# Third head's query one position later in the first head, and the first latents' head's query products behind the weighted sums of positions five and six

## The chip, the core and the metric

The kernel runs on one core of a Trainium2 chip. Its engines work through queues of their own, in the order written in the program, and wait for each other by semaphores: TensorE (PE, matmuls and their weight loads PEld), VectorE (DVE), ScalarE (ACT), GpSimd (POOL, which here issues the gathers) and SyncE (SP, which issues the other transfers). The metric is the time of one execution in microseconds of the device; less is better.

## The reference

One layer of a backbone over 128 context tokens and 512 latent tokens, D = 1024: a modulated RMS norm, a mixer (state space and short convolution), a residual, and then the part in which the change lies, a retrieval of single-neuron experts:

```python
def block(xb):                                   # 128 tokens
    q = (xb @ w_query).reshape(TOKEN_BLOCK, PEER_HEADS, 2, PEER_DQ // 2)
    s = jnp.einsum("thse,sne->thsn", q, sk)      # scores of 2 x 128 keys
    s1, i1 = lax.top_k(s[:, :, 0], PEER_TOPK)
    s2, i2 = lax.top_k(s[:, :, 1], PEER_TOPK)
    cand = s1[..., :, None] + s2[..., None, :]   # 16 x 16 sums
    ...
    top, pos = lax.top_k(cand, PEER_TOPK)
    idx = jnp.take_along_axis(cidx, pos, axis=-1)
    gate = jax.nn.softmax(top, axis=-1)
    hid = jnp.einsum("thkd,td->thk", expert_u[idx], xb)
    act = jax.nn.gelu(hid) * gate
    return jnp.einsum("thk,thkd->td", act, expert_v[idx])
```

There are 8 heads, 16 experts for each token and head, and five blocks of 128 tokens: the context and four of latents. The context's block runs first.

## The kernel before

After a first part of some 210 us (modulation, mixer of the context, scans) one long loop does the retrieval: `for G in range(NALL)`, 40 turns, one for each block and head, G = 8 b + head. In this text "first head" is G = 0, "seventh head" G = 6, and so on. Each turn has 8 positions g, and each position handles two of a token's 16 experts. Every engine has the same double loop, written out by hand, and what stands in it sets the order of its queue.

- **GpSimd** (L1861) gathers one expert row for each of 128 tokens, 8 KB each (the u half and the v half together), into one of 8 row slots. It waits for the experts of the head (`topk_done`) and for its slot, which is free when the weighted sum of the expert 8 places before is done (`v_done`). The sum of position g frees two slots, so the sums of positions 4 to 7 admit the first eight gathers of the next head.
- **VectorE**: for each expert k, `dot` (L1678) multiplies the row's u half with the token; every second k, `weigh` (L1690) writes the weights of the position before. Between them stand the stages of the next head's top-k, from `best_keys` (L1619, top keys, ahead of dot 0, it waits for the key scores) to `take_experts` (L1663, ahead of dot 8, in the first head dot 10), which reads what TensorE has spread, and, in the first eight heads, the latents' mixer (`latent_front`, among them L1725 and L1739). The weight of position 7 is written in the next head, behind its top keys and dot 0.
- **ScalarE**: a Gelu for each position (L1228), and the evictions of query and scores: `take_q`, `take_scores` (L1203, L1209) for the context's heads, `take_q_lat`, `take_scores_lat` (L1213 to L1220) for the latents'.
- **TensorE**: at each position `add_rows` (L846), the weighted sum of two experts' v halves; `spread_experts` (L832); `latent_front` (L908 to L934) for the latents' mixer in the first six heads; and the query of the head after the next, u = G + 2, in two halves (`query`, L781; `query_lat`, L814) and its key scores (`scores`, L801; `scores_lat`, L823). For the latents one query head serves all 512 tokens; the first of these is u = 8, in the seventh head. It needs the latents' normed tokens, which ScalarE's modulation (L1082) finishes in position 4 of that head.
- **SyncE** loads w_query head by head into one buffer: the next load waits until both halves of the query before have been computed. The tiles of the latents' weights stand in the same queue.

The position in which a query half stands is fixed by `g in (3, 4)` and `g in (4, 5)` in the loops: it stands ahead of the position's weighted sum. The scores stand in position 6.

Of the kernel before, what the change touches and what calls it, by code (L numbers as in the profile page):

```python
# [37 lines left out]
HEADS = 8  # L38
# [41 lines left out]
def build(nc, xT, condT, cols, w_mod, w_u, w_tiles, w_o, ssm, bc, dskip, skT, w_query, table, y_out, st_out, kfull):  # L80
    ctx = ExitStack()
    with ctx:
# [276 lines left out]
        NQC = 2 * HEADS  # L359
# [122 lines left out]
        def _(pe):  # L482
# [171 lines left out]
            for i in range(4):  # L654
                for term in range(5):
                    r = (term - 1) // 2
                    for a in range(2):
                        for j in range(4):
                            g = 8 * j + 2 * i + a
# [115 lines left out]
            def query(u, halves=range(2)):  # L775

                pe.wait_ge(ld_wq, 16 * u)
                pe.wait_ge(sc_ev, u)
                for h in halves:
                    for k in range(KD):  # L780
                        last = mm(bank[2][:, h * P:(h + 1) * P], wqb[:, k, h * P:(h + 1) * P], hT[:, k, 0:CTX], start=(k == 0), stop=(k == KD - 1))  # L781
                if h == 1:
                    last.then_inc(q_mm, 1)
# [33 lines left out]
            def scores_lat(u):  # L817

                n = u - HEADS
                pe.wait_ge(lq_ev, 2 * n + 2)  # L820
                for j in range(4):
                    for h in range(2):
                        last = mm(bank[2 + j // 2][:, (j % 2) * DQ + h * P:(j % 2) * DQ + (h + 1) * P], qTl[:, h, j * P:(j + 1) * P], sk[:, h, :],  # L823
                                  start=True, stop=True)
                last.then_inc(sc_mm, 1)
# [187 lines left out]
            for G in range(NALL):  # L1013
                b, head = G // HEADS, G % HEADS
                t, u = G + 1, G + 2
                for g in range(NPR):
                    if g == (2 if G else 4) and t < NALL:
                        spread_experts(t)
                    if u < HEADS:
                        if g in (3, 4):  # L1020
                            query(u, (g - 3,))
                        if g == 6:
                            scores(u)
                    if HEADS <= u < NQC:
                        if g in (4, 5):
                            query_lat(u, g - 4)
                        if g == 6:
                            scores_lat(u)
                    add_rows(G, g)
                    if G == 0 and g == 0:  # L1030
                        turn_y(2)
                        turn_y(3)
                    if b == 0:
                        latent_front(NPR * G + g)
                    if head == HEADS - 1 and b < NBLK - 1:
                        if g == 1:
                            turn_rows(b + 1)
                        for tg in HID_AT.get(g, ()):
                            select_group(b + 1, tg)
                    if head == 0 and b and g == 2:  # L1040
                        turn_sums(b - 1)
                    if head == 1 and b and g == 1:
                        final_squares(b - 1)
                    if G == NALL - 5 and g in (1, 3):
                        last_rows(g // 2)
# [5 lines left out]
        def _(act):  # L1051
# [273 lines left out]
            for G in range(NALL):  # L1325
                b, head = G // HEADS, G % HEADS
                e, t, u = G % 2, G + 1, G + 2
                for g in range(NPR):
                    if g == (1 if G else 3) and t < NALL:
                        exps(t)  # L1330
                    if u < HEADS:
                        if g == 5:
                            take_q(u)
                        if g == 6:
                            take_scores(u)
                    gelu(G, e, g)
                    if G == 0 and g == 0:
# [2 lines left out]
                    if b == 0:  # L1340
                        latent_front(NPR * G + g)
                    if HEADS <= u < NQC:
                        if g in (4, 5):
                            take_q_lat(u, g - 4)
                        if g == 6:
                            take_scores_lat(u)
                    if head == HEADS - 1 and b < NBLK - 1:
                        if g == 2:
# [577 lines left out]
```

## Time and profile before

| | us |
|---|---|
| timed executions, median of 3 (1967.2 to 1967.95) | 1967.68 |
| profiled execution, whole | 1977.83 |
| its span, first to last instruction | 1976.0 |
| TensorE busy (61%) | 1196.6 |
| VectorE busy (73%) | 1441.2 |
| ScalarE busy (19%) | 375.7 |
| GpSimd busy (36%) | 719.9 |

The gathers move 671.13 of the 745.90 MB; the slices in the second half of the span show 413 to 421 GB/s, mostly near 417, but for the last. TensorE's mean granted clock is 0.699. The profile knows each instruction by line, engine and operation, with the time it started, how long it took, and in brackets how long its engine had been idle before and what released it. In windows each engine has its busy time and count, then come the granted TensorE clock (1.00 is 2.4 GHz, 0.50 is 1.2 GHz), the DMA share and GB/s. A matmul of the program shows as two in the trace.

### The profile page before, as it was taken

Reading aid. Unit: us, or ns where it says so; the run is one execution under the profiler, and the core shown is the slowest. Engines: PE = TensorE matmul, PEld = TensorE weight load, DVE = VectorE, ACT = ScalarE, POOL = GpSimd, SP = SyncE. Lnnn points to the kernel's source line nnn. Section 1 sums busy time; section 2 is a strip of 40 time slices with the busy share of each in tenths; the row PEclk is TensorE's granted clock in tenths of the full one; section 3 lists DMA queues with packets and bytes.
Section 4 is the critical chain, followed back from the end, with each engine's and each line's share of the span. In section 5 each row is a group of like instructions: output and inputs, shape, how many; then the busy total and the mean of one; then the engine's idle time right before and its main releaser. Section 6 shows DMA issues by size and latency. Waiting matters only on the chain.

```text
span 1976.0 us, 22252 instructions
## 1 busy us (share of the span) xinstructions
PE 1196.6 (61%) x7540; PEld 460.7 (23%) x7540; DVE 1441.2 (73%) x3894; ACT 375.7 (19%) x845; POOL 719.9 (36%) x666
## 2 busy tenths in 40 slices
PE   6999888988767666775544434464434454444444
PEld 3569533333323222221101000021000011011001
DVE  8977566877766776666788777777777777876765
ACT  5232431221222111111221011121111111211110
POOL 0000332333333433433443444444344444344442
PEclk9999998999878777776655555565555566555555
DMA  8556799999989999999999999999999999999996
GB/s 347 173 202 227 279 367 344 377 376 387 396 330 384 389 397 388 397 403 372 420 417 421 421 414 416 420 407 419 413 413 419 410 413 410 416 417 411 414 417 255
DMA packets 126242, 745.90 MB, mean 377 GB/s; under 512 B 12128, under 2 KB 34912, under 8 KB 40624
## 3 DMA queue, kind: packets, MB, share of 16 engines
q0 software_dynamic: 92160, 671.13, 83.2%
q1 hardware_dynamic: 33968, 73.35, 10.4%
q8 instruction: 59, 0.97, 0.2%
q14 instruction: 55, 0.45, 0.1%
HBM read 741.78 MB, written 2.65 MB: 377 GB/s over the span
## 4 chain that ended last, share of the span: by engine, by line
DMA 34%; PE 29%; DVE 24%; issue 10%; ACT 1%; SPq 0%; DVEq 0%; POOL 0%; POOLq 0%; ACTq 0%
DMA r<-table,gidx 30%; DVE r L1678 8%; PE bank L846 7%; PE bank L814 6%; DMA r<-w_query 3%; PE bank L923 3%; PE bank L934 2%; PE bank L543 2%; DMA r<-w_u 2%; DVE wgt L1690 1%; PE bank L781 1%; DVE r L1646 1%; DVE i L1620 1%; DVE i L1626 1%; DVE r L1621 1%
## 5 line engine op out<-in xcount | busy, mean ns | idle before, releaser
L1861 POOL DMA_INDIRECT r<-table,gidx x640 | 711.7, 1112 | 1072.8 <-PE bank L846 911.2
L1678 DVE CUSTOM_DVE_ANT_0 r<-r 128x1024 f32<-128x1024 f32 x640 | 780.0, 1224 | 302.7 <-DMA r<-table,gidx 273.9
L846 PE MATMUL bank<-r,wgt 128*32 128x512 f32 x2560 | 536.0, 923 | 729.3 <-DVE wgt L1690 710.5
L846 PEld LDWEIGHTS bank<-r,wgt 128*32 128x32 f32 x2560 | 61.5, 131 | 1103.4 <-DVE wgt L1690 1033.6
L1228 ACT ACTIVATE r<-r 128x2 f32<-128x2 f32 x320 | 65.1, 203 | 1046.5 <-DVE r L1678 1038.6
L814 PE MATMUL bank<-hT_r,r 128*128 128x512 f32 x256 | 123.6, 639 | 0.9 <-ACT hT_r L1082 0.9
L1687 DVE TENSOR_TENSOR r<-r 128x2 f32<-128x2 f32 x320 | 50.1, 157 | 92.3 <-ACT r L1228 92.3
L1690 DVE TENSOR_TENSOR wgt<-fold,r 128x64 f32<-128x64 f32 x320 | 72.0, 225 | 11.1
L814 PEld LDWEIGHTS bank<-hT_r,r 128*128 128x128 f32 x256 | 51.3, 206 | 77.6 <-issue 77.6
L1228 ACT ACT_TABLE_LOAD x51 | 65.4, 1283 | 0.9
L923 PE MATMUL bank<-hT_r,r 128*128 128x512 f32 x128 | 62.2, 631 | 0.0
L934 PE MATMUL bank<-mix_r,r 128*128 128x512 f32 x128 | 61.2, 621 | 0.0
L832 PEld LDWEIGHTS bank<-r,ident 128*32 128x32 f32 x1280 | 43.0, 139 | 48.8 <-DVE r L1657 42.7
L1678 DVE DVE_READ_ACCUMULATOR2_ANT r<- 128x1 f32 x640 | 52.9, 83 | 0.0
L1224 ACT ACT_TABLE_LOAD x40 | 51.3, 1283 | 0.7
L871 PE MATMUL bank<-mix_r,modrow 128*128 128x512 f32 x80 | 48.0, 737 | 3.2 <-ACT r L1243 1.9
L832 PE MATMUL bank<-r,ident 128*32 128x8 f32 x1280 | 46.8, 195 | 3.9 <-DVE r L1657 3.6
L1846 POOL MEMSET r<- 128x2048 f32 x1 | 1.8, 1813 | 93.2 <-DVE sv L1477 93.2
L1619 DVE MAX8 r<-r 128x8 f32<-128x128 f32 x80 | 19.3, 284 | 22.0 <-ACT r L1220 15.9
L1224 ACT ACTIVATE r<-r,small 128x16 f32<-128x16 f32 x40 | 12.3, 308 | 119.9 <-DVE pos L1639 119.9
L781 PE MATMUL bank<-hT_r,r 128*128 128x128 f32 x224 | 29.5, 289 | 7.2 <-DMA r<-w_query 7.2
L543 PE MATMUL bank<-hT_r,r 128*128 128x512 f32 x64 | 32.0, 646 | 2.2 <-DMA r<-w_u 2.2
(356 smaller groups left out, 1431.4 us busy)
## 6 DMA issues: line engine op xcount, KB each, us to landing
r<-w_mod SPq DMA_DIRECT2D x24, 1024.0 KB, 8.4
r<-w_query SPq DMA_DIRECT2D x15, 1024.0 KB
r<-table,gidx POOLq DMA_INDIRECT x640
r<-w_tiles SPq DMA_DIRECT2D x12, 512.0 KB, 6.7
x_r<-w_tiles SPq DMA_DIRECT2D x10, 512.0 KB, 5.8
hT_r<-xT SPq DMA_DIRECT2D x4, 640.0 KB, 6.2
r<-w_u SPq DMA_DIRECT2D x1, 2048.0 KB, 30.5
r<-w_o SPq DMA_DIRECT2D x1, 2048.0 KB, 11.1
```

The lines of the kernel that those rows point to most:

```text
L543: last = mm(bank[m][:, :], wu[:, k, m * P:(m + 1) * P], hT[:, k, CTX:T], start=(k == 0), stop=(k == KD - 1))
L814: last = mm(bank[2 + h][:, :], wqb[:, k, h * P:(h + 1) * P], hT[:, k, CTX:T], start=(k == 0), stop=(k == KD - 1))
L832: last = mm(bank[3][TG * s:TG * s + TG, 8 * tg:8 * tg + 8], ident[:, TG * tg:TG * tg + TG], gi[:, :, 4 * s:4 * s + 4], start=True, stop=True)
L846: last = mm(bank[ACC[b % 2][h]][to:to + TG, :], wgt[:, g % 2, e, :], rows[:, k % SLOTS, D + h * 512:D + (h + 1) * 512], start=(G % HEADS = ...
L923: last = mm(bank[(4, 5, 7)[r]][:, :], wtl[(tile + 2) % 3][:, k, :], hT[:, k, CTX:T], start=(k == 0), stop=(k == KD - 1))
L934: last = mm(bank[OUT_BANK[m % 3]][:, :], woA[:, m % 4, k, :], mixl[:, k, :], start=(k == 0), stop=(k == KD - 1))
L1224: A(e16, top, ACT.Exp, bias=small[:, 0:1], accum_out=small[:, 1:2]).then_inc(exp_done, 1)
L1228: A(gel[:, par, 2 * g:2 * g + 2], hid[:, par, 2 * g:2 * g + 2], ACT.Gelu_apprx_tanh).then_inc(gelu_done, 1)
L1678: V.tensor_tensor_reduce(rows[:, s, 0:D], rows[:, s, 0:D], h2r[tg], 1.0, 0.0, ALU.mult, ALU.add, hid[:, par, k:k + 1]).then_inc(dot_done, 1)
L1687: wl(tt(a, a, gate[:, par, 2 * g:2 * g + 2], ALU.mult))
L1690: tt(wgt[:, g % 2, :, :], fold[:, :].rearrange("p (a m) -> p a m", a=1).broadcast_to([P, 2, TG]), a.rearrange("p (g m) -> p g m", m=1).bro ...
L1861: G_.indirect_dma_start(rows[:, k % SLOTS, :], None, table, bass.IndirectOffsetOnAxis(gidx[:, e, k:k + 1], 0)).then_inc(row_in[k % SLOTS], 16)
```

## The change

Two things move, on TensorE and on ScalarE. In the first head the halves of the third head's query (u = 2) go from positions 3 and 4 to 4 and 5, its eviction from 5 to 6, its scores and their eviction from 6 to 7. In the seventh head the halves of the first latents' query (u = 8) go from ahead of the sums of positions 4 and 5 to behind those of 5 and 6, the scores from position 6 to 7; ScalarE takes the two halves in positions 6 and 7, behind the Gelus of these, and the scores in 7. Other heads keep their places, and no instruction is added or left out.

```diff
                     if u < HEADS:
-                        if g in (3, 4):
-                            query(u, (g - 3,))
-                        if g == 6:
+                        q0 = 3 if G else 4
+                        if g in (q0, q0 + 1):
+                            query(u, (g - q0,))
+                        if g == q0 + 3:
                             scores(u)
-                    if HEADS <= u < NQC:
+                    if HEADS < u < NQC:
                         if g in (4, 5):
                             query_lat(u, g - 4)
                         if g == 6:
                             scores_lat(u)
+                    if u == HEADS and g == 7:
+                        scores_lat(u)
                     add_rows(G, g)
+                    if u == HEADS and g in (5, 6):
+                        query_lat(u, g - 5)
...
                     if u < HEADS:
-                        if g == 5:
+                        q0 = 3 if G else 4
+                        if g == q0 + 2:
                             take_q(u)
-                        if g == 6:
+                        if g == q0 + 3:
                             take_scores(u)
...
                     if HEADS <= u < NQC:
-                        if g in (4, 5):
-                            take_q_lat(u, g - 4)
-                        if g == 6:
+                        q0 = 4 if u > HEADS else 6
+                        if g in (q0, q0 + 1):
+                            take_q_lat(u, g - q0)
+                        if g == max(q0 + 1, 6):
                             take_scores_lat(u)
```

TensorE's queue in the first head, before, from the product of position 2 (L908) to that of position 4 (L912, L923); L781 is a query half, L846 a weighted sum, L832 the spreading of the experts:

```order
L908 MATMUL bank<-r 128x512 [waits sgl_ev]
L908 MATMUL bank<-r 128x512 x3
L781 MATMUL bank<-hT_r,r 128x128 [waits sc_ev,ld_wq]
L781 MATMUL bank<-hT_r,r 128x128 x7
L846 MATMUL bank<-r,wgt 32x512 [waits wgt_ready]
L846 MATMUL bank<-r,wgt 32x512 x3
```

The difference at the same place, of the changed kernel against the one before, at the scores (L801):

```order
 L912 MATMUL bank<-r,ones 128x512 [waits sql_ready]
 L923 MATMUL bank<-hT_r,mix_r 128x512 x4
-L801 MATMUL bank<-sk,r 128x128 [waits q_ev]
-L801 MATMUL bank<-sk,r 128x128
 L846 MATMUL bank<-r,wgt 32x512 [waits wgt_ready]
 L846 MATMUL bank<-r,wgt 32x512 x3
```

Of the first piece the two L781 rows are gone in the changed kernel, so the sum of position 3 follows the product of position 2; the halves now follow the products of positions 3 and 4. The scores leave their place ahead of the sum of position 6 and stand ahead of that of position 7.

TensorE's queue in the seventh head, before, from the first half (L814) to the scores (L823):

```order
L814 MATMUL bank<-hT_r,r 128x512 [waits h_ready,sc_ev,ld_wq]
L814 MATMUL bank<-hT_r,r 128x512 x7
L846 MATMUL bank<-r,wgt 32x512 [waits wgt_ready]
L846 MATMUL bank<-r,wgt 32x512 x3
L814 MATMUL bank<-hT_r,r 128x512 [waits topk_done]
L814 MATMUL bank<-hT_r,r 128x512 x7
L846 MATMUL bank<-r,wgt 32x512 [waits wgt_ready]
L846 MATMUL bank<-r,wgt 32x512 x3
L823 MATMUL bank<-sk,r 128x128 [waits lq_ev]
L823 MATMUL bank<-sk,r 128x128 x7
```

And in the changed kernel, from the sums of positions 4 and 5 to the scores:

```order
L846 MATMUL bank<-r,wgt 32x512 [waits wgt_ready]
L846 MATMUL bank<-r,wgt 32x512 x3
L846 MATMUL bank<-r,wgt 32x512 [waits wgt_ready]
L846 MATMUL bank<-r,wgt 32x512 x3
L814 MATMUL bank<-hT_r,r 128x512 [waits h_ready,sc_ev,ld_wq]
L814 MATMUL bank<-hT_r,r 128x512 x7
L846 MATMUL bank<-r,wgt 32x512 [waits wgt_ready]
L846 MATMUL bank<-r,wgt 32x512 x3
L814 MATMUL bank<-hT_r,r 128x512 [waits topk_done]
L814 MATMUL bank<-hT_r,r 128x512 x7
L823 MATMUL bank<-sk,r 128x128 [waits lq_ev]
L823 MATMUL bank<-sk,r 128x128 x7
```

Two sums stand ahead of the first half, one between the halves, and none between the second half and the scores, which wait for ScalarE's eviction of that half (`lq_ev`).

ScalarE's queue in the seventh head, before, from the last modulation (L1082); L1213 takes a half, L1228 is a Gelu, L1217 begins the eviction of the scores:

```order
L1082 ACTIVATE hT_r<-hT_r,modT,gs 128x512
L1213 ACTIVATE r<-bank 128x512 [waits lq_mm]
L1228 ACTIVATE r<-r 128x2 [waits dot_done]
L1213 ACTIVATE r<-bank 128x512 [waits lq_mm]
L1228 ACTIVATE r<-r 128x2 [waits dot_done]
L1217 ACTIVATE r<-bank 128x512 [waits sc_mm]
```

The same in the changed kernel, where these lines are five further down:

```order
L1087 ACTIVATE hT_r<-hT_r,modT,gs 128x512
L1233 ACTIVATE r<-r 128x2 [waits dot_done] x2
L1218 ACTIVATE r<-bank 128x512 [waits lq_mm]
L1233 ACTIVATE r<-r 128x2 [waits dot_done]
L1218 ACTIVATE r<-bank 128x512 [waits lq_mm]
L1222 ACTIVATE r<-bank 128x512 [waits sc_mm]
```

The Gelus of positions 5, 6 and 7 each go ahead of an eviction that they followed before.

## Rows read from the trace of the kernel before

**Rows 1.** The page: DMA share by slice; the chain that ended last, by line.

```profile
DMA  8556799999989999999999999999999999999996
...
DMA r<-table,gidx 30%; DVE r L1678 8%; PE bank L846 7%; PE bank L814 6%; DMA r<-w_query 3%; PE bank L923 3%; PE bank L934 2%; PE bank L543 2%; DMA r<-w_u 2%; DVE wgt L1690 1%; PE bank L781 1%; DVE r L1646 1%; DVE i L1620 1%; DVE i L1626 1%; DVE r L1621 1%
```

**Rows 2.** First head, TensorE: start us, busy us, line, [idle before <- releaser].

```profile
243.65 3.70 PE L908 MATMUL bank<-r 128*128 128x512 f32 x8
251.62 2.80 PE L781 MATMUL bank<-hT_r,r 128*128 128x128 f32 x16 [4.27 <-DMA r<-w_query]
254.35 1.93 PE L846 MATMUL bank<-r,wgt 128*32 128x512 f32 x8
...
259.84 0.88 PE L832 MATMUL bank<-r,ident 128*32 128x8 f32 x32
...
262.67 1.07 PE L846 MATMUL bank<-r,wgt 128*32 128x512 f32 x8
...
268.15 1.07 PE L846 MATMUL bank<-r,wgt 128*32 128x512 f32 x8
...
273.54 0.61 PE L801 MATMUL bank<-sk,r 128*128 128x128 f32 x4
...
280.65 1.06 PE L846 MATMUL bank<-r,wgt 128*32 128x512 f32 x8
```

**Rows 3.** First head, VectorE: a weight, experts taken, top keys, product.

```profile
248.08 0.23 DVE L1690 TENSOR_TENSOR wgt<-fold,r 128x64 f32<-128x64 f32 x1
...
260.75 0.17 DVE L1663 COPY r<-bank 128x16 f32<-128x16 f32 x1 [10.70 <-PE bank L832]
...
276.18 0.48 DVE L1619 MAX8 r<-r 128x8 f32<-128x128 f32 x2
...
286.32 0.69 DVE L1739 TENSOR_TENSOR r<-r,bank 128x512 f32<-128x512 f32 x1 [0.42 <-PE bank L923]
```

**Rows 4.** First head, windows: busy by engine, granted clock, DMA share, GB/s.

```profile
253.00:254.00 1.00, 1.00 (x6) 1.00 (x6) 0.00 (x0) 0.00 (x0) 0.00 (x0) 0.50 1.02 422
254.00:269.00 15.00, 15.00 (x92) 6.54 (x91) 7.87 (x18) 3.70 (x6) 5.45 (x4) 0.93 0.80 289
```

**Rows 5.** Seventh head, TensorE in order of time.

```profile
562.18 9.37 PE L814 MATMUL bank<-hT_r,r 128*128 128x512 f32 x16 [0.95 <-ACT hT_r L1082]
571.48 1.06 PE L846 MATMUL bank<-r,wgt 128*32 128x512 f32 x8
...
580.54 2.05 PE L823 MATMUL bank<-sk,r 128*128 128x128 f32 x16
...
587.37 1.93 PE L846 MATMUL bank<-r,wgt 128*32 128x512 f32 x8 [3.78 <-DVE wgt L1690]
```

**Rows 6.** Seventh head, VectorE in order of time.

```profile
561.64 0.23 DVE L1690 TENSOR_TENSOR wgt<-fold,r 128x64 f32<-128x64 f32 x1
...
564.60 1.23 DVE L1678 CUSTOM_DVE_ANT_0 r<-r 128x1024 f32<-128x1024 f32 x1 [1.60 <-DMA r<-table,gidx]
...
583.87 0.49 DVE L1619 MAX8 r<-r 128x8 f32<-128x128 f32 x2 [1.94 <-ACT r L1220]
```

**Rows 7.** Seventh head, ScalarE: second eviction of the query.

```profile
579.65 0.60 ACT L1213 ACTIVATE r<-bank 128x512 f32<-128x512 f32 x1 [7.37 <-PE bank L814]
```

**Rows 8.** Seventh head, window from the first query half into the second.

```profile
570.00:577.50 7.50, 7.50 (x24) 2.92 (x23) 2.67 (x6) 0.69 (x2) 2.30 (x2) 1.00 0.52 188
```

**Rows 9.** Eighth head, TensorE: the tenth head's two query halves.

```profile
608.63 7.03 PE L814 MATMUL bank<-hT_r,r 128*128 128x512 f32 x16
...
618.40 7.03 PE L814 MATMUL bank<-hT_r,r 128*128 128x512 f32 x16
```

**Rows 10.** Eighth head, window behind the second half.

```profile
625.00:627.50 2.50, 1.83 (x11) 0.46 (x10) 0.30 (x2) 1.67 (x4) 0.28 (x1) 1.00 0.56 215
```

**Rows 11.** Eighth head, VectorE: a dot product that waits for rows.

```profile
612.31 1.23 DVE L1678 CUSTOM_DVE_ANT_0 r<-r 128x1024 f32<-128x1024 f32 x1 [2.39 <-DMA r<-table,gidx]
```

**Rows 12.** Twelfth head, TensorE: a first query half behind the fourth sum.

```profile
793.06 8.30 PE L814 MATMUL bank<-hT_r,r 128*128 128x512 f32 x16
```

## The prediction

> **What bounds the kernel now.** I read the page first. Its DMA strip stands at 9 from the sixth of its 40 slices on, but for the last and the twelfth, which holds the seventh head. The chain that ended last is 30% gathers of table rows, but TensorE's weighted sums (L846) and query halves (L814) are 7% and 6% of the span on it [rows 1]. So I looked at who waits for whom at the two places the change touches, and not at the sums over the span.
>
> In the first head the two query halves of the third head stand in TensorE's queue behind the products of positions two and three. The first half waits 4.27 us for the load of w_query, with the sum of position three queued behind it [rows 2], although that sum's weight was written at 248.3 us [rows 3]. The idle time costs again afterwards: the granted clock is 0.50 in 253 to 254 us, the 1.2 GHz level [rows 4], and the half takes 2.80 us. VectorE meanwhile stands 10.70 us before it can take the next head's experts [rows 3], since their spreading comes only at 259.84 us [rows 2].
>
> In the seventh head VectorE does not wait for rows at the end: it waits for the key scores. The first query half of the ninth head starts at 562.18 us, released by ScalarE's modulation, and from there TensorE runs without a gap through sum 4, half two, sum 5 and the scores at 580.54 [rows 5]. ScalarE takes the scores, VectorE starts the top keys at 583.87 [rows 6], and the weight of sum 7 stands behind these top keys and one dot product, so sum 7 starts at 587.37 [rows 5]. VectorE then never waits for rows up to the eighth head's sum 3, and TensorE goes on from there into the query halves at 608.63 and 618.40 [rows 9]. **That is one unbroken chain** from 562 to 625 us; what delays the first half delays everything behind it. The gathers are not its bound: between 570 and 577.5 us the DMA share is only 0.52 [rows 8].
>
> **Place one, the first head.** The two halves go one position later, the key scores from position six to seven, and ScalarE's evictions with them. I walk the new queue with the old durations. Sum 3 starts at 248.4 (weight at 248.3 [rows 3]) and takes 1.0; the product of position three takes 3.70 [rows 2], end 253.1. Spreading and one half took 2.83 (259.84 to 262.67 [rows 2]): end 255.9. VectorE takes the experts at 254.0 instead of 260.75 and needs 1.9 to the weight (it did so in the trace, sum 4 at 262.67 being ready then), so sum 4 starts at 256.0, against 262.67. Its latent product (262.67 to 268.15 is sum plus product, 5.5) ends at 261.4, the second half 2.0 later at 263.4, sum 5 with its product 5.4 later (268.15 to 273.54 [rows 2]) at 268.9, sum 6 with its product 5.5 later at 274.4, and then the scores. They stood at 273.54 and now stand at 274.4: **the 4.27 us of idle and 1.6 us of slow clock are saved, but the product of position six, 4.5 us, now runs ahead of the scores.** The scores end at 275.0, ScalarE copies in 0.5, VectorE starts the top keys at 275.5, against 276.18 [rows 3], where it was held by a dot product. Sum 7 stands behind the top keys, a dot product and its weight; from the start of the top keys to sum 7 the seventh head has 3.5 (583.87 to 587.37 [rows 5, 6]), so it starts at 279.0 against 280.65. TensorE idles 4.0 us for it, nearly as long as the gap that was followed by the 0.50 clock [rows 2, 4], and that gap cost 1.6 or 1.7 (2.80 on the half against 2.0, 1.93 on the sum against 1.07). So the product that VectorE waits for at 286.32 [rows 3] comes at 280.65 − 1.65 + 1.65 + its 5.5, just when it came before: **place one comes out even, 0.0 us**. Ends: −1.1 if the clock stays high (VectorE's own chain is 0.7 early and its 0.42 wait goes), +1.5 if the slow stretch covers all of the product (3.70 at the high clock). I take 0.0, since the gap is nearest to the 4.27 us one. The next load of w_query and the weight tiles are released by the same products and come some 4 us earlier on SP; nobody waited for them there.
>
> The Trainium skill ("TensorE: Matmul & The Clock Gate", section "Loop structure matters more than you think") says that a wait between bursts of matmuls drops the clock to half. The 0.50 clock after the 4.27 us wait agrees. By it the change trades one such gap for another; without it place one would give −1.1 and the sum 1971.2.
>
> **Place two, the seventh head.** Sums 4 and 5 now stand ahead of the first half. Sum 4 has its weight at 561.9 [rows 6] and takes 1.9 at the low clock. Sum 5 needs the dot products of rows 10 and 11, a Gelu, and, by VectorE's order, the dot product of row 12, which waits for its gather until 564.60 and ends at 565.8 [rows 6]; its weight is there at 566.2. Sum 5 ends at 568.2. **The first half starts there, 6.0 us later than 562.18.** It may be shorter than 9.37, since TensorE has worked before it: in the twelfth head, where sum 3 runs at the low clock right ahead of it and no half waits for a modulation, it took 8.30 [rows 12]. That is −1.1, with ends 0 (9.37 again [rows 5]) and −2.3 (7.03, as in the eighth head [rows 9]). Between the first half and the scores stood two sums and one half, 571.48 to 580.54 or 9.1 us [rows 5]; now stand one sum (1.0), one half (7.1), and ScalarE's copy of the second half, 0.60 [rows 7] and 0.1 of handing over, which sum 5 used to cover: 8.8, so −0.3. The sum is 6.0 − 1.1 − 0.3 = **+4.6 us** at the scores, bounds +3.4 and +5.7. Scores, their copy, the top keys, one dot product and the weight up to sum 7 stay 6.8 us (580.54 to 587.37 [rows 5]): sum 7 starts at about 592.0.
>
> What is won there: sums 4 and 5 free row slots 7 and 11 us earlier, so six of the eighth head's gathers are early and the empty DMA stretch at 572 fills. But sums 6 and 7 come at 576.5 and 592.0 instead of 582.52 and 587.37, and the gathers behind sum 7 with them; between these the DMA runs dry instead. ScalarE's Gelus of positions five to seven no longer stand behind the evictions, yet VectorE only idles longer before the scores.
>
> **Sum.** 0.0 + 4.6 = +4.6 us on a span of 1976.0 us, 1.83 us of the 1977.83 us of the profiled execution lying around it. The timed ones have a median of 1967.68, 10.15 us less; the difference is carried over unscaled: 1967.68 + 4.6 = **1972.3 us**, 0.23% slower. Behind the tenth head's halves the DMA share is again only 0.56 [rows 10]: few gathers are outstanding there in either order, so from there on everything is the same but later, and a delay is carried on as it is.
>
> **Rivals.** *The DMA alone counts, and it gets faster.* The share is 0.80 over 254 to 269 [rows 4] and 0.52 over 570 to 577.5 [rows 8]: 15 × 0.20 + 7.5 × 0.48 = 3.0 + 3.6 = 6.6 us of empty DMA. If early gathers fill that and stay ahead to the end, the time is 1967.68 − 6.6 = 1961.1. It decides if the backlog built in the early gathers outlasts the wait for sum 7. Six gathers cannot: a gather is 128 rows of 8 KB, 1.05 MB, which is 2.5 us at the 417 GB/s of the full slices, so six are through by some 587 and sum 7's two are asked for at 594. The Trainium skill ("Perfetto Trace Analysis", section "Identifying the Most-Contended Engine") says to improve the most contended engine first; that is this rival's rule with the DMA as that engine. The trace speaks against it here: while the share is 0.52, VectorE waits for ScalarE and TensorE, not for rows [rows 6]. Chance 0.11.
>
> *The delay of place two is absorbed.* In the eighth head VectorE waits for rows, 2.39 us for one of them [rows 11], so it could be 4.6 us late and lose little; 0 to 2 us would be left, say 1.1, 1968.8. Against it: the path to the tenth head's halves [rows 9] leads over sum 3, which does not wait for rows. Chance 0.16.
>
> *Place one keeps its whole saving.* If the scores were not behind a product, 4.3 + 1.6 = 5.9 us would be saved there, total +4.6 − 5.9, 1966.4. Chance 0.07.
>
> *More slow clock*: +1.5 and +5.7 at the two places, and some more where a shifted head meets the low clock: beyond 1975, to 1978. Chance 0.08.
>
> **How the numbers follow.** The forecast has 0.58; its own range is −1.1 + 3.4 = +2.3 to 1.5 + 5.7 = +7.2, so 1970.0 to 1974.9. A measurement of this kernel tells 0.2%, 3.9 us, from no change, so the part of the forecast below 1971.6, a fourth of it, falls to "same". Faster: 0.11. Same: 0.16 + 0.07 + 0.14 = 0.37. Slower: 0.44 + 0.08 = 0.52. The range 1966 to 1976 leaves out the first rival and the far end of the last, about 0.15.
>
> **What would show it.** Place one: sum 3 at 248.4, experts taken at 254, the scores of the third head near 274.4 and an idle gap of 4 us before sum 7 at 279.0, with a clock of 0.50 shortly behind. Place two: sum 5 done at 568, the first half at 568 to 576.5, scores at 585, top keys at 588.5, sum 7 at 592, all shifted by what place one gives; a dry DMA near 588 to 594. It would be wrong if the tenth head's halves did not start some 4.6 us later than 608.63 and 618.40 [rows 9]; if they are later and the end is not, the second rival has it further on.

## The result

The changed kernel takes 1980.03 us (median of 7, 1972.81 to 1981.72), the kernel before 1967.95 (median of 7, 1966.73 to 1971.14). The ratio is **1.0044, 95% interval 1.0028 to 1.0061**, which is +8.7 us (5.5 to 12.0) on 1967.95. It is slower, as the likeliest case had it, but by about twice the forecast 4.6 us, and the median lies 4 us above the range. The profiled execution took 1980.33 us, its span is 1978.5 us. All ratios of this document are of fast runs; one slow execution of the kernel before, 5193.41 us in the last series, is left out of them.

The page of the changed kernel: clock and DMA by slice, then the chain that ended last, by line:

```profile
PEclk9999998999978777776655555565555566555555
...
DMA  8456798999998999999999999999999999999996
...
DMA r<-table,gidx 30%; DVE r L1685 8%; PE bank L846 7%; PE bank L814 6%; PE bank L923 3%; PE bank L934 2%; PE bank L543 2%; DMA r<-w_query 2%; DVE wgt L1697 1%; PE bank L781 1%; DVE r L1653 1%; DVE i L1627 1%; DVE r L1628 1%; DVE i L1633 1%; DVE pos L1641 1%
```

Against [rows 1] nearly nothing moves: a share of 1% is 20 us here, so the page cannot show this change. The hollow in the DMA strip's twelfth slice stands in the thirteenth (593 to 643 us). The two places have to be read row by row. (In the changed kernel VectorE's lines are 7 higher, L1697 writes the weights and L1685 is the dot product; ScalarE's are 5 higher.)

**First head**, TensorE in order of time:

```profile
251.01 1.06 PE L846 MATMUL bank<-r,wgt 128*32 128x512 f32 x8 [1.02 <-DVE wgt L1697]
...
256.45 2.05 PE L781 MATMUL bank<-hT_r,r 128*128 128x128 f32 x16
263.86 1.95 PE L781 MATMUL bank<-hT_r,r 128*128 128x128 f32 x16
...
273.18 3.60 PE L923 MATMUL bank<-hT_r,r 128*128 128x512 f32 x8
276.61 0.61 PE L801 MATMUL bank<-sk,r 128*128 128x128 f32 x4
281.56 1.93 PE L846 MATMUL bank<-r,wgt 128*32 128x512 f32 x8 [4.34 <-DVE wgt L1697]
283.42 2.08 PE L912 MATMUL bank<-r,ones 128*128 128x512 f32 x2
285.29 4.10 PE L923 MATMUL bank<-hT_r,r 128*128 128x512 f32 x8
```

The wait for w_query of [rows 2] is gone. The product of position six stands ahead of the scores (L801), TensorE then idles 4.34 us for the weight behind the top keys. The sum that follows and the first part of its product (L912 in 2.08 us for 1.13, L923 in 4.10 for 3.60) run at the low clock. The window shows it (busy by engine, clock, DMA share, GB/s), where [rows 4] had the same behind the wait for w_query:

```profile
281.00:285.00 4.00, 3.44 (x10) 1.04 (x11) 3.62 (x16) 1.05 (x2) 0.72 (x1) 0.50 0.99 375
```

**Seventh head**, TensorE, to be set beside [rows 5]:

```profile
564.16 1.94 PE L846 MATMUL bank<-r,wgt 128*32 128x512 f32 x8 [0.68 <-DVE wgt L1697]
568.31 1.94 PE L846 MATMUL bank<-r,wgt 128*32 128x512 f32 x8 [2.21 <-DVE wgt L1697]
570.17 8.53 PE L814 MATMUL bank<-hT_r,r 128*128 128x512 f32 x16
578.63 1.06 PE L846 MATMUL bank<-r,wgt 128*32 128x512 f32 x8
579.63 7.13 PE L814 MATMUL bank<-hT_r,r 128*128 128x512 f32 x16
587.45 2.05 PE L823 MATMUL bank<-sk,r 128*128 128x128 f32 x16 [0.69 <-ACT r L1218]
594.28 1.93 PE L846 MATMUL bank<-r,wgt 128*32 128x512 f32 x8 [4.78 <-DVE wgt L1697]
```

VectorE at its top keys, beside the 1.94 us of [rows 6], and the windows over the first half (0.52 in [rows 8]) and between scores and sum 7:

```profile
590.79 0.49 DVE L1626 MAX8 r<-r 128x8 f32<-128x128 f32 x2 [14.16 <-ACT r L1225]
```

```profile
587.00:594.00 7.00, 2.05 (x16) 1.86 (x16) 2.93 (x14) 1.54 (x4) 0.00 (x0) 0.96 0.75 281
570.00:577.50 7.50, 7.50 (x18) 3.33 (x15) 4.00 (x8) 0.20 (x1) 3.14 (x3) 0.80 1.01 423
```

The early gathers fill the empty stretch (0.52 becomes 1.01), and VectorE, with its rows in place, idles 14.16 us for the scores. The emptiness has moved: the share is 0.75 in 587 to 594 us and 0.84 over 593 to 643, where the kernel before has 1.02 in 587 to 594 and 0.97 over 594 to 643. The filled stretch is worth little, because the head ends when the scores come.

### The profile page after: what moved, and what is told of

It is laid out like the page before. It is cut to its first block, busy times and chain, and to the rows that moved or that the text cites. A ratio compares the mean times of both kernels' runs of the same rounds, so it can differ in the third digit from the quotient of the medians.

```text
span 1978.5 us, 22252 instructions
## 1 busy us (share of the span) xinstructions
PE 1200.5 (61%) x7540; PEld 461.9 (23%) x7540; DVE 1441.6 (73%) x3894; ACT 376.5 (19%) x845; POOL 720.4 (36%) x666
## 4 chain that ended last, share of the span: by engine, by line
DMA 32%; PE 30%; DVE 25%; issue 11%; ACT 2%; POOL 0%; DVEq 0%; POOLq 0%; SPq 0%; ACTq 0%
DMA r<-table,gidx 30%; DVE r L1685 8%; PE bank L846 7%; PE bank L814 6%; PE bank L923 3%; PE bank L934 2%; PE bank L543 2%; DMA r<-w_query 2%; DVE wgt L1697 1%; PE bank L781 1%; DVE r L1653 1%; DVE i L1627 1%; DVE r L1628 1%; DVE i L1633 1%; DVE pos L1641 1%
## 5 line engine op out<-in xcount | busy, mean ns | idle before, releaser
L1685 DVE CUSTOM_DVE_ANT_0 r<-r 128x1024 f32<-128x1024 f32 x640 | 780.1, 1224 | 307.2 <-DMA r<-table,gidx 289.8
L846 PE MATMUL bank<-r,wgt 128*32 128x512 f32 x2560 | 539.8, 928 | 735.6 <-DVE wgt L1697 716.9
L846 PEld LDWEIGHTS bank<-r,wgt 128*32 128x32 f32 x2560 | 61.6, 130 | 1112.6 <-DVE wgt L1697 1043.3
L814 PE MATMUL bank<-hT_r,r 128*128 128x512 f32 x256 | 118.7, 618 | 0.0
L1697 DVE TENSOR_TENSOR wgt<-fold,r 128x64 f32<-128x64 f32 x320 | 72.0, 225 | 11.1
L814 PEld LDWEIGHTS bank<-hT_r,r 128*128 128x128 f32 x256 | 49.5, 199 | 73.1 <-issue 73.1
L923 PE MATMUL bank<-hT_r,r 128*128 128x512 f32 x128 | 62.5, 633 | 0.0
L832 PEld LDWEIGHTS bank<-r,ident 128*32 128x32 f32 x1280 | 43.5, 140 | 48.9 <-DVE r L1664 42.7
L1685 DVE DVE_READ_ACCUMULATOR2_ANT r<- 128x1 f32 x640 | 52.9, 83 | 0.0
L871 PE MATMUL bank<-mix_r,modrow 128*128 128x512 f32 x80 | 48.8, 748 | 3.2 <-ACT r L1248 1.9
L832 PE MATMUL bank<-r,ident 128*32 128x8 f32 x1280 | 47.4, 196 | 3.7 <-DVE r L1664 3.6
L1229 ACT ACTIVATE r<-r,small 128x16 f32<-128x16 f32 x40 | 12.4, 309 | 121.4 <-DVE pos L1646 121.4
L923 PEld LDWEIGHTS bank<-hT_r,r 128*128 128x128 f32 x128 | 24.7, 202 | 38.9 <-issue 38.9
L934 PEld LDWEIGHTS bank<-mix_r,r 128*128 128x128 f32 x128 | 23.7, 195 | 38.3 <-issue 36.6
```

The source lines that it names most:

```text
L814: last = mm(bank[2 + h][:, :], wqb[:, k, h * P:(h + 1) * P], hT[:, k, CTX:T], start=(k == 0), stop=(k == KD - 1))
L832: last = mm(bank[3][TG * s:TG * s + TG, 8 * tg:8 * tg + 8], ident[:, TG * tg:TG * tg + TG], gi[:, :, 4 * s:4 * s + 4], start=True, stop=True)
L846: last = mm(bank[ACC[b % 2][h]][to:to + TG, :], wgt[:, g % 2, e, :], rows[:, k % SLOTS, D + h * 512:D + (h + 1) * 512], start=(G % HEADS = ...
L871: last = mm(bank[at[h]][:, :], modrow[:, tg // 2, tg % 2 * P:(tg % 2 + 1) * P], h2tok[:, 512 * h:512 * h + 512], start=True, stop=True)
L923: last = mm(bank[(4, 5, 7)[r]][:, :], wtl[(tile + 2) % 3][:, k, :], hT[:, k, CTX:T], start=(k == 0), stop=(k == KD - 1))
L934: last = mm(bank[OUT_BANK[m % 3]][:, :], woA[:, m % 4, k, :], mixl[:, k, :], start=(k == 0), stop=(k == KD - 1))
```

## The experiments

All are read with one ruler: the start of the weighted sum (L846) of each position. "Step 0.2" is the time from the start of sum 2 of the first head to that of sum 3; "first head" is from sum 0 of the first head to sum 0 of the second. A second ruler is the timed ratio to the kernel before, taken on the same chip. Segments in us, spans of the traced executions:

```
trace           first heads  seventh heads    span
                head  2 - 6   head  8 - 14
before          55.5  253.1   54.1   321.1   1976.0
again_before    56.0  248.6   54.5   321.4   1972.6
before_trace    52.9  246.6   54.1   318.0   1967.0
before_trace2   54.6  249.8   53.7   318.7   1969.1
place1_only     56.1  251.8   54.6   319.3   1975.4
place1_trace    59.9  248.7   54.6   319.1   1976.7
place1_trace2   57.5  251.6   54.8   318.5   1976.3
place2_only     54.2  249.1   58.8   318.5   1972.2
place2_trace    50.7  252.3   58.5   316.9   1973.1
after           57.4  252.1   58.8   314.9   1978.5
again_after     57.5  248.7   59.1   315.1   1971.6
after_trace2    56.8  249.3   58.6   317.0   1976.2
after_trace3    55.9  252.1   58.7   318.0   1978.6
scores_late     62.2  246.6   54.0   317.4   1972.5
halves_late     56.0  250.3   54.3   319.4   1973.8
halves_q6       51.8  251.4   54.1   321.0   1971.3
half_behind4    52.8  246.0   54.9   318.5   1966.4
early_both      51.8  250.8   55.1   315.1   1968.5
```

From the fifteenth head to the end all 18 take 1061.0 to 1063.4 us: what is lost or won by then stays so.

**The two kernels again**, unedited, as the yardstick.

> The kernel before itself, for a second trace and for what the measurement tells from no change. Both theories: ratio 1.000, interval within 0.2%. If the profiled execution of before was a long one (1977.83 against a median of 1967.95), this trace has a span near 1966, and the 10 us lie in the tenth to fourteenth heads, where the two traces at hand come back together by 6.3 us. If they are the profiler's, the span is near 1976 again.

> The changed kernel itself again. Theory A (the delay at place two, 4.7 us in the trace, is carried to the end and nothing else costs): +5 us, 1973. Theory B (the first measurement holds, +8.7 us or more: something behind place two costs again): 1976 to 1980.

Measured: the kernel before against itself 1971.64 to 1968.39, 1.0013 (0.9999 to 1.0026); the changed one 1983.59 to 1968.39, 1.0069 (1.0047 to 1.0092). The loss is real, and on this chip larger than either theory had it (1973, or 1976 to 1980). The expectation for the kernel before failed too: its span is 1972.6 us for 1966, and heads 8 to 14 take 321.4 us, no less than in the first trace, so the long execution is not long there. The kernel before ran from 1962.96 to 1976.51 us in 23 executions, so a single trace is off the median by up to 8 us in either direction.

**Each place alone.**

```diff
 # place1_only: the first-head part of the change (ScalarE's part of it too)
-                        if g in (3, 4):
-                            query(u, (g - 3,))
-                        if g == 6:
+                        q0 = 3 if G else 4
+                        if g in (q0, q0 + 1):
+                            query(u, (g - q0,))
+                        if g == q0 + 3:
                             scores(u)
...
 # place2_only: the seventh-head part (ScalarE's part of it too)
+                    if u == HEADS and g == 7:
+                        scores_lat(u)
                     add_rows(G, g)
+                    if u == HEADS and g in (5, 6):
+                        query_lat(u, g - 5)
```

> Only the first head's part, the third head's query one position later; the seventh head as before. Forecast of the prediction: 0.0 us, -1.1 to +1.5. Rival (it keeps its saving of idle): -3 us or more. Theory B with its cost here: +3 to +4 us.

> Only the seventh head's part, the first latents' query behind sums five and six. Forecast: +4.6 us. If absorbed: 0 to +2. If its delay puts the later heads into a longer rhythm, +7 to +10.

Measured: place one alone 1977.23 to 1968.39, **1.0051** (1.0033 to 1.0069); place two alone 1974.29, **1.0029** (1.0015 to 1.0042). Place two costs +5.7 us, and its interval (3.0 to 8.3) holds the forecast 4.6. Place one, forecast at 0.0, costs +10.0 us (6.5 to 13.6). That is the miss.

**Which part of place one.** Two runs split it: the halves late but the scores only one position behind the eviction, and the scores late alone.

```diff
 # halves_late (scores stay at 6, ScalarE's take_q at 5)
-                        if g in (3, 4):
-                            query(u, (g - 3,))
+                        q0 = 3 if G else 4
+                        if g in (q0, q0 + 1):
+                            query(u, (g - q0,))
...
 # scores_late, on TensorE and ScalarE
-                        if g == 6:
+                        if g == (6 if G else 7):
```

> The first head's query halves one position later as in the change, but the scores and their eviction stay in position 6; ScalarE takes the query in position 5; seventh head as before. Theory A (what costs at place one is the product that now runs ahead of the scores): the scores come 4 us earlier than in the changed kernel, the first head's end 3 to 5 us before that of the kernel before, ratio 0.998. Theory B (what costs is the halves or the earlier transfers behind them): slower, as the first head's part alone was, 1.005.

> Only the third head's scores and their eviction move from position 6 to 7 of the first head, the halves stay where they were. Theory A: this has the whole cost and none of the saving, so sum 0 of the second head comes 4 to 6 us later than in the kernel before, ratio 1.003 to 1.005. Theory B: no change in time.

Measured: halves_late 1975.28 to 1971.09, 1.0017 (1.0003 to 1.0031); scores_late 1973.96, 1.0018 (1.0004 to 1.0032). Neither ratio is one that a theory named: halves_late was to be 0.998 or 1.005, scores_late 1.003 to 1.005 or no change. The two losses are little larger than the 1.0013 between two series of one kernel, so the traces have to decide. The late scores give the longest first head of all, 62.2 us, and leave the wait for w_query where it was. TensorE there:

```profile
252.49 3.38 PE L781 MATMUL bank<-hT_r,r 128*128 128x128 f32 x16 [4.90 <-DMA r<-w_query]
...
279.87 0.61 PE L801 MATMUL bank<-sk,r 128*128 128x128 f32 x4
284.82 1.93 PE L846 MATMUL bank<-r,wgt 128*32 128x512 f32 x8 [4.34 <-DVE wgt L1690]
```

The 4.34 us gap and the low clock come from the scores standing behind the product of position six: here the halves are in their old places, and both are there. From sum 3 to sum 0 of the second head it takes 37.3 us for 31.3, the 4 to 6 us of Theory A. halves_late has a price of its own. On ScalarE the eviction of the query waits for the second half and holds back the Gelu of position five behind it (L1229), which also pays 1.28 us for a table load. VectorE's weight comes late and sum 5 waits 2.44 us; the product behind it is 1.7 us longer than in halves_q6 below, at the low clock:

```profile
265.98 0.38 ACT L1204 ACTIVATE r<-bank 128x256 f32<-128x256 f32 x1 [8.89 <-PE bank L781]
266.38 1.28 ACT L1229 ACT_TABLE_LOAD   x1
267.67 0.20 ACT L1229 ACTIVATE r<-r 128x2 f32<-128x2 f32 x1
```

**Both costs taken out of place one.** Halves at 4 and 5 as in the change, scores ahead of sum 6, and ScalarE takes the query in position six, behind the Gelu of position five, as in the change:

```diff
 # halves_q6: halves_late, and
-                        if g == 5:
+                        if g == (5 if G else 6):
                             take_q(u)
```

> First head only: the query halves in positions 4 and 5, the scores stay in position 6 ahead of its sum, and ScalarE takes the query in position 6 too, so no Gelu stands behind a half. Theory A (place one costs because the scores wait for one more product and sum 7 for them): this has no such wait, sum 0 of the first head to sum 0 of the second takes 50 to 53 us where the changed kernel's traces have 57 and those of before 53 to 56; ratio 0.997 to 1.000. Theory B (any later half costs, through what it does to the transfers): 1.003 or more.

Measured 1968.87 to 1969.89, 0.9997 (0.9985 to 1.0009): the loss of place one is gone, the halves are as late as in the change. TensorE:

```profile
272.92 1.06 PE L846 MATMUL bank<-r,wgt 128*32 128x512 f32 x8 [1.02 <-DVE wgt L1691]
...
278.41 1.07 PE L846 MATMUL bank<-r,wgt 128*32 128x512 f32 x8
...
283.89 1.06 PE L846 MATMUL bank<-r,wgt 128*32 128x512 f32 x8
```

With the scores ahead of sum 6, that sum and its product cover VectorE's top keys. The gap is 1.02 us and the clock stays high (1.00 over 270 to 284 us). This is Theory A's first head (51.8 us for 50 to 53) and its ratio; Theory B's 1.003 lies outside the interval.

**A dose for place two.** The first half behind sum 4 only, the second behind sum 5, the scores back at position six:

```diff
 # half_behind4 (the halves leave their place ahead of the sums; ScalarE takes them in 5 and 6)
...
                     add_rows(G, g)
+                    if u == HEADS and g in (4, 5):
+                        query_lat(u, g - 4)
```

> Seventh head only, half as far as the change: the first query half behind sum 4, the second behind sum 5, scores in position 6 ahead of sum 6, ScalarE takes the halves behind the Gelus of 5 and 6. By the walk of the prediction the scores come 1.3 us later than before, where the change has 4.7. Chain theory: ratio 1.0005. Rival (the seventh head's empty DMA counts): faster, since sum 4 frees its slots 7 us early and there is no wait for sum 7.

Measured 1970.27 to 1971.09, 1.000 (0.9984 to 1.0016). The seventh head takes 54.9 us, 0.5 more than the old order's 54.3:

```profile
553.48 1.94 PE L846 MATMUL bank<-r,wgt 128*32 128x512 f32 x8 [0.69 <-DVE wgt L1694]
555.34 8.81 PE L814 MATMUL bank<-hT_r,r 128*128 128x512 f32 x16
564.08 1.07 PE L846 MATMUL bank<-r,wgt 128*32 128x512 f32 x8
565.07 7.13 PE L814 MATMUL bank<-hT_r,r 128*128 128x512 f32 x16
572.89 2.05 PE L823 MATMUL bank<-sk,r 128*128 128x128 f32 x16 [0.69 <-ACT r L1216]
```

Sum 4's weight is there after an idle 0.69 us. The half behind it starts 24.6 us after the head's start, 1.6 later than in [rows 5], and takes 8.81 us for 9.37; the scores are 0.8 us late (42.1 for 41.3), where 1.3 were expected. Sum 5's weight comes 4.15 us after sum 4 starts (564.16 to 568.31 in the changed kernel), and a half that stands behind it pays for that: in the changed kernel the first half starts 28.7 us after the head's start. So it is mainly the wait for sum 5 that costs, as the chain has it. (The second half and the scores are one position earlier here too, so the run does not part these from the first half.)

**More traces**, to see how much of one trace is that execution.

> The kernel before again, one look for a third trace. The timed executions of it have a median near 1968, the two traces at hand 1974 and 1978. If the traced ones are drawn from the same executions, this one is near 1968, and the place where it is shorter shows where executions of one kernel differ: the steps between weighted sums that differ by 2 us or more between traces (fourth head, positions 2 to 3, and second head, 2 to 3).

> The kernel before, a fourth trace. If a wait for w_query ahead of sum 3 and a low clock right behind sum 0 exclude each other, this trace has one of them: either a wait of 2 to 4 us and 54 to 56 us for the first head, or none, the product of position 0 at the low clock, and about 53 us and a span near 1967.

> The first head's part alone, a second trace. Theory A: from sum 0 of the first head to that of the second 56 to 58 us, 2 to 4 more than before, whatever the clock does; the heads behind, whose code is unchanged, 249 to 252 us up to the seventh as in the first trace and both of the changed kernel's. If these are chance alone, they may be at 246.

> The seventh head's part alone, a second trace. The seventh head 58.8 us against 54.1 to 54.5 of before in every trace; the seven heads behind it 315 to 319 us against 318 to 321: a part of the delay is given back there. If it isn't, 320.

> The changed kernel, one more look. If the loss of place one lies in the first head alone: from the first weighted sum of head one to that of head two 56 to 60 us (the kernel before 51 to 56), steps after sums 3, 4, 5 and 6 of 7.27, 5.49, 10.34 and 7.8 to 8.2 us whatever the time of the execution; heads two to six 246 to 253 us as in the kernel before, the seventh 58.8, heads 8 to 14 315 to 318. If executions above 1980 us hold a further loss, it shows as a segment outside these bounds.

> The changed kernel again, for the same question: the same steps in the first and the seventh head to within 0.5 us, and whatever differs between this execution and the others outside them is the spread of the unchanged heads (in the kernel before, 246.0 to 253.1 us for heads two to six).

> The move in the first head alone. First head 56 to 60 us, seventh head 54.1 to 54.6, heads 8 to 14 318 to 321. If the loss beyond +4 us lies in heads two to six, these stand above 250 us here too; if it is the spread of executions, they fall anywhere from 246 to 253.

These executions took 1968.83, 1970.86, 1978.45, 1974.95, 1978.00, 1980.43 and 1978.11 us. Most segments fall where they were expected; outside by over 0.3 us are the first head of place1_trace (59.9 us for 56 to 58) and step 0.7 of after_trace2 (7.17 for 7.8 to 8.2). The steps of the first head settle place one (old order: the four traces of before, two with place two alone, half_behind4; place one: seven traces):

```
step                     0.2                                 0.3        0.4   0.5    0.6       0.7
old order   6.41 6.41 6.41 9.49 10.11 11.70 12.52   7.45 to 8.39   5.48  7.02   5.48      5.49
place one   5.71 in all seven                       7.45           7.27  5.49  10.34  7.17 to 8.18
```

Steps 0.3 to 0.7 are the same in all seven traces with place one, but for the last, and together 7.1 us longer than in the old order (38.4 against 31.3). What pays for it is step 0.2, and that differs from execution to execution: in three of seven old-order traces the query half does not wait for w_query at all. In the trace of before that took 1968.83 us, TensorE in order of time, and a window:

```profile
233.74 1.94 PE L846 MATMUL bank<-r,wgt 128*32 128x512 f32 x8 [3.30 <-DVE wgt L1690]
...
238.84 5.92 PE L908 MATMUL bank<-r 128*128 128x512 f32 x8 [1.27 <-ACT r L1249]
...
253.85 1.95 PE L781 MATMUL bank<-hT_r,r 128*128 128x128 f32 x16
255.73 1.07 PE L846 MATMUL bank<-r,wgt 128*32 128x512 f32 x8
```

```profile
234.00:244.00 10.00, 8.73 (x23) 3.85 (x16) 9.29 (x28) 3.32 (x4) 1.86 (x2) 0.53 1.05 404
```

Here the clock falls early, behind sum 0, and products zero and one end later. That looks like the reason why the half finds w_query loaded, but it is not: the load itself was quick. From its issue to its landing the load of w_query took 15.9 us in this trace, so it landed near 244.3 us, 9.5 before the half, and the slow stretch is 3.6 us. The two other traces without a wait have 16.9 and 18.1 us. In the trace of before that took 1970.86 us the load took 25.4 us. The load in the two traces of before (issue, size, us from issue to landing):

```profile
r<-w_query SPq DMA_DIRECT2D x1, 1024.0 KB, 15.9
r<-w_query SPq DMA_DIRECT2D x1, 1024.0 KB, 25.4
```

In the second of these both stand together, a low clock behind sum 0 and a wait for w_query, which the expectation had as excluding each other; place two's second trace has a slow sum 0 and no wait. TensorE in these two traces:

```profile
230.16 1.91 PE L846 MATMUL bank<-r,wgt 128*32 128x512 f32 x8 [3.30 <-DVE wgt L1690]
...
250.28 3.40 PE L781 MATMUL bank<-hT_r,r 128*128 128x128 f32 x16 [2.09 <-DMA r<-w_query]
```

```profile
233.66 1.94 PE L846 MATMUL bank<-r,wgt 128*32 128x512 f32 x8 [3.30 <-DVE wgt L1697]
...
251.54 1.95 PE L781 MATMUL bank<-hT_r,r 128*128 128x128 f32 x16
```

The wait for a slow load can cover a slow stretch behind sum 0, as in the first of these two traces. Once the load is quick the stretch is a loss in either order: steps 0.0 of 8.72 and 10.96 us go with first heads of 50.7 and 52.9 us in the old order, and place1_trace, with 10.90, has the longest first head of its seven, 59.9 us. Why one load takes 16 us and another 25 was not tested.

**Both mended places together**, halves_q6 and half_behind4 in one kernel.

> First head: halves one position later, but the scores stay behind sum 6 and ScalarE takes the query behind the Gelu of position 6, so no product stands between. Seventh head: first latents' first half behind sum 4, second behind sum 5. Theory of the chain: first head 52 to 55 us, seventh 54.5 to 55.5, time within 0.15% of the kernel before (1966 to 1973 where it has 1969). Rival, in which any later query or earlier latent half costs by itself: over 0.3% slower. Rival, in which freeing position 3 pays: over 0.15% faster.

As in halves_q6, the scores stand ahead of sum 6 and ScalarE takes the query behind the Gelu of position five; the expectation names their places wrongly. Measured 1969.94 to 1970.87, 0.9993 (0.9981 to 1.0006); first head 51.8, seventh 55.1. The chain's theory holds: with both costs taken out, the whole loss is gone. No kernel here beats the one before by more than can be measured.

## Why the prediction was right and wrong

**What bounds the kernel: right.** Both places are paid in scores that come late, not in gathers. The DMA rival fails as the prediction argued: the empty stretch was filled (0.52 to 1.01), the DMA ran dry behind it, and the kernel got slower. (The full slices of the kernel before run from 407 to 421 GB/s, not from 413; a gather's 2.5 us stands.)

**Place two: right, step by step.** In the changed trace the seventh head begins 2.25 us later than in the trace of before (541.47 against 539.22). With that added, the forecast has sum 5 at 568.4, the first half at 570.4, the scores at 587.4 and sum 7 at 594.2; the rows say 568.31, 570.17, 587.45 and 594.28, the half 8.53 us long for 8.3. The tenth head's halves, the forecast's own test, start 74.07 and 83.85 us after the seventh head's start for 69.41 and 79.18 in [rows 9]: 4.7 late. TensorE there:

```profile
615.54 7.03 PE L814 MATMUL bank<-hT_r,r 128*128 128x512 f32 x16
...
625.32 7.03 PE L814 MATMUL bank<-hT_r,r 128*128 128x512 f32 x16
```

Over all traces the seventh head is 58.7 us (six) for 54.3 (seven without place two): +4.4.

**"A delay is carried on as it is": not borne out by the traces.** Heads 8 to 14 take 316.7 us with place two (mean of six, 314.9 to 318.5) for 319.4 (seven, 318.0 to 321.4): some 2.7 us come back. Of these 2.2 are in the tenth head, positions 1 to 3. Before (the trace of 1968.83 us), then changed, TensorE and one row of VectorE each:

```profile
685.70 2.70 PE L886 MATMUL bank<-r,ones 128*128 128x128 f32 x16
...
690.76 1.29 DVE L1678 CUSTOM_DVE_ANT_0 r<-r 128x1024 f32<-128x1024 f32 x1 [1.13 <-DMA r<-table,gidx]
692.45 1.06 PE L846 MATMUL bank<-r,wgt 128*32 128x512 f32 x8 [2.36 <-DVE wgt L1690]
693.44 8.83 PE L814 MATMUL bank<-hT_r,r 128*128 128x512 f32 x16
```

```profile
698.39 3.78 PE L886 MATMUL bank<-r,ones 128*128 128x128 f32 x16
...
703.24 0.17 DVE L1670 COPY r<-bank 128x16 f32<-128x16 f32 x1 [1.22 <-PE bank L832]
705.15 1.06 PE L846 MATMUL bank<-r,wgt 128*32 128x512 f32 x8 [1.07 <-DVE wgt L1697]
706.15 7.13 PE L814 MATMUL bank<-hT_r,r 128*128 128x512 f32 x16
```

Three things add up here. The short products ahead (L886) run at the low clock, 3.78 us for 2.70, and that step is 1.3 us longer. The wait for the weight of sum 3 is shorter, that step by 1.8 us: VectorE waits 0.3 us for rows on the way to sum 3 (mean of the six) where it waited 1.8 (the seven). And the query half takes 7.13 us for 8.83, that step is 1.7 us shorter. So part of the delay is absorbed by VectorE's waits for rows, as the second rival had it, though in the tenth head and not in the eighth, which takes 48.2 to 48.8 us with and without place two. The quick half is another matter: early_both has it too, behind quick products (2.66 us) and with a seventh head only 0.7 us longer. Why was not tested.

**Place one: the term that failed.** The walk from sum 3 on was right: sum 3 to sum 0 of the second head was worked out at 37.7 us and measures 38.3 in the changed trace, with the gap (4.34 for 4.0) and the low clock behind it, which costs 1.7 to 2.7 us over the seven traces for 1.65. What was mis-sized is the saving set against it. The step took the wait and slow half of [rows 2], 4.3 + 1.6 us, as what every execution pays. (The step is the sentence "the 4.27 us of idle and 1.6 us of slow clock are saved".) Step 0.2 falls from 11.70 to 5.71 in the profiled execution, 6.0 us, but over the seven old-order traces from a mean of 9.0, 3.3 us, with 0.7 in the three whose load of w_query was quick. So place one is +7.1 − 3.3 = **+3.8 us in place of 0.0**. In the pair of profiled executions alone it is near the forecast: the first head takes 57.4 us for 55.5, and 1.3 of that is step 0.0. The trace said itself that it was unusual: 1977.83 us, 10 above the median. The forecast carried that difference over as a constant when part of it was the very wait the change removes.

**The sum.** Four traces of the changed kernel against four of before: +2.5 us at the start of the second head, +1.1 in heads 2 to 6, +4.7 in the seventh, −3.6 in 8 to 14, +0.4 behind: +5.1, the difference of the mean spans (1976.2 and 1971.2) within rounding. That this is near the forecast 4.6 is luck, a loss at place one that was not forecast and a return behind place two. The timed difference is +8.7. The four traced executions of before lie 3.7 us above the medians of their series (1972.98 for 1969.33), those of the changed kernel average 1978.0, below its medians of 1980.03 and 1983.59, and no trace shows a loss at a third place. **Three things stay open.** The timed loss is larger than what the steps hold: at place one alone +3.8 us, where the timed interval begins at 6.5, and at place two 4.4 − 2.7 = +1.7, where it begins at 3.0. That the whole loss goes with the two costs (early_both) shows their cause and not how it adds up. Heads 2 to 6, whose code is the same, are 250.6 us in the seven traces with place one (248.7 to 252.1) and 249.3 in the seven without (246.0 to 253.1); the two shortest are old-order, but the ranges overlap. And executions of 1983 to 1987 us, four of the six in again_after, were never caught in a trace.

Of the other rivals, "place one keeps its whole saving" fails on the scores behind a product; "more slow clock" (to 1978) is nearest in the number, but the low clock gave only 0.7 us more than forecast at place one (step 0.7, mean of seven), and at place two the half took 8.53 us for 8.3.

## What to carry to other kernels

When the profiled execution is well off the median of the timed ones, look at a second and third before a saving is read out of it: a wait that only some executions have is worth its mean, while a cost that is built into the order is paid in all of them. Before a query product is moved later, ask which work covers the top keys behind its scores; here one sum and its product (5.5 us) did, and moving the scores past them cost more than the wait for w_query. If a product has to move behind a sum, put it behind one whose weight is already there.

## What the runs showed of the hardware

The same gap did not bring the same clock. TensorE idles 3.30 us ahead of the first head's sum 0 in every trace. What it did ahead of that is the same too (scores in 0.71 us, L896 in 1.04). Behind the gap the sum takes 1.06 or 1.07 us at clock 1.00 in five of the 18 executions (the trace of [rows 2] and place1_only among them), and 1.48 to 1.94 in the others, where up to 3.6 us are lost until sum 1 (step 0.0: 7.39 to 10.96). Place one alone, sum 0 in the two cases:

```profile
231.53 1.06 PE L846 MATMUL bank<-r,wgt 128*32 128x512 f32 x8 [3.30 <-DVE wgt L1692]
```

```profile
232.75 1.94 PE L846 MATMUL bank<-r,wgt 128*32 128x512 f32 x8 [3.30 <-DVE wgt L1692]
```

The Trainium skill ("TensorE: Matmul & The Clock Gate", section "Loop structure matters more than you think") has a long wait for the DMA between matmuls drop the clock to half. The 4.34 us gap, a wait for VectorE, agrees: in six of the seven traces with place one the sum behind it takes 1.93 or 1.94 us, in the seventh 1.07, and there the loss on the product behind it is smaller (step 0.7 of 7.17). The 3.30 us gap agrees in some executions of one kernel and not in others, while the half behind a wait of only 2.09 us took 3.40 us for 1.95, at clock 0.50 from 251 to 253 us; here the measurement decides. The load of w_query, 1 MB, took from 15.9 to 25.4 us from issue to landing in traces of one kernel.
